# Two pairs of modulation units instead of one in three output passes, and six more half product units

## The reference

```
mod = silu(c) @ w_mod[l] + b_mod[l]                    # 9 x 1024 values for each layer, once for c, once for c_ctx
h   = rmsnorm(x, ng[0]) * (1 + m(1)) + m(0)
gu  = h @ ffn_wi                                       # 1024 -> 2 * 2816
x   = x + 0.5 * m(2) * rmsnorm((silu(gu[:, :2816]) * gu[:, 2816:]) @ ffn_wo, ng[1])
```

## Time and profile before

| | |
|---|---|
| median of 3 runs | 3053.07 us (3049.8 to 3058.28) |
| the profiled execution | 3051.59 us |
| its span, first to last instruction | 3049.8 us |
| TensorE busy | 2910.4 us (95%) |
| VectorE busy | 2166.0 us (71%) |
| ScalarE busy | 1294.8 us (42%) |
| mean granted TensorE clock | 0.981 of full speed |

### The profile page before, as it was taken

One profiled execution on the slowest core, in us unless ns is written; L12 is line 12 of the kernel. 1 busy time (PEld: TensorE's weight loads), 2 busy tenths in 40 slices (PEclk: granted clock), 3 DMA queues, 4 the chain that ended last, 5 costly groups with the idle time before them and its releaser, 6 DMA issues.

```text
span 3049.8 us, 62386 instructions
## 1 busy us (share of the span) xinstructions
PE 2910.4 (95%) x26152; PEld 2601.7 (85%) x26152; DVE 2166.0 (71%) x3223; ACT 1294.8 (42%) x2165; POOL 416.7 (14%) x465
## 2 busy tenths in 40 slices
PE   6999999999988899999999999999998889999998
PEld 5999878996777689998799998799876777999986
DVE  4987586756666788876878776767566767787635
ACT  3135454235533451454532554532454435345434
POOL 1000111002333220001100001110033333100100
PEclk8999999999989999999999999999998999999999
DMA  6522444410000244225452225453010004312234
GB/s 250 201 70 84 152 153 152 179 46 27 30 4 14 99 173 166 70 70 187 145 193 90 90 70 200 145 177 130 15 52 8 3 13 161 111 70 84 83 124 172
DMA packets 92915, 325.10 MB, mean 107 GB/s; under 512 B 10288, under 2 KB 13936, under 8 KB 77296
## 3 DMA queue, kind: packets, MB, share of 16 engines
q1 hardware_dynamic: 92656, 321.39, 29.7%
HBM read 318.05 MB, written 3.31 MB: 105 GB/s over the span
## 4 chain that ended last, share of the span: by engine, by line
PE 80%; DVE 10%; ACT 3%; issue 3%; DMA 3%; POOL 0%; SPq 0%; ACTq 0%; DVEq 0%; POOLq 0%
PE PS L2606 22%; PE PS L2672 20%; PE PS L2719 18%; PE PS L2616 3%; PE PS L812 2%; DMA wo<-in_wo 2%; PE PS L1584 2%; PE PS L836 1%; PE PS L1563 1%; DVE wo_lo L3131 1%; ACT wo_hi L2838 1%; PE PS L759 1%; PE PS L1576 1%; DMA wm<-in_wm 1%; PE PS L824 1%
## 5 line engine op out<-in xcount | busy, mean ns | idle before, releaser
L2606 PE MATMUL PS<-h_hi,wi_hi 128*128 128x384 f32 (+2 forms) x1632 | 406.8, 311 | 11.2 <-issue 11.2
L2719 PE MATMUL PS<-wo_hi,a_hi 128*128 128x512 f32 x968 | 391.6, 405 | 19.3 <-DVE wo_lo L3131 12.7
L2606 PE MATMUL PS<-h_hi,wi_lo 128*128 128x384 f32 (+2 forms) x1632 | 403.8, 309 | 0.0
L2606 PE MATMUL PS<-h_lo,wi_hi 128*128 128x384 f32 (+2 forms) x1632 | 403.7, 309 | 0.0
L3131 DVE TENSOR_TENSOR wo_lo<-wo,wo_hi 128x1024 fp32r<-128x1024 f32 x208 | 255.4, 1228 | 193.2 <-ACT wo_hi L2838 192.6
L2719 PE MATMUL PS<-wo_hi,a_lo 128*128 128x512 f32 x968 | 378.6, 391 | 0.0
L2719 PE MATMUL PS<-wo_lo,a_hi 128*128 128x512 f32 x968 | 378.0, 390 | 0.0
L2838 ACT ACTIVATE wo_hi<-wo 128x1024 fp32r<-128x1024 f32 x208 | 220.2, 1059 | 304.8 <-PE PS L2719 206.6
L3191 DVE TENSOR_TENSOR part_lo<-wi,part_hi 128x512 fp32r<-128x512 f32 x378 | 255.5, 689 | 105.2 <-ACT part_hi L2872 102.2
L2872 ACT ACTIVATE part_hi<-wi 128x512 fp32r<-128x512 f32 x378 | 236.1, 630 | 190.5 <-PE PS L2672 118.8
L2606 PEld LDWEIGHTS PS<-h_hi,wi_hi 128*128 128x128 f32 (+1 forms) x1632 | 262.4, 188 | 15.4 <-issue 13.4
(11 more groups left out here) (370 smaller groups left out, 5813.2 us busy)
## 6 DMA issues: line engine op xcount, KB each, us to landing
wi<-in_wi SPq DMA_DIRECT2D x88, 1024.0 KB, 4.8
wo<-in_wo SPq DMA_DIRECT2D x176, 512.0 KB, 3.2
wm_in<-in_wm SPq DMA_DIRECT2D x104, 512.0 KB, 3.7
wi<-in_win SPq DMA_DIRECT2D x24, 1024.0 KB, 5.2
wo<-in_wout SPq DMA_DIRECT2D x32, 512.0 KB, 3.2
wm_out<-in_wm SPq DMA_DIRECT2D x24, 512.0 KB, 4.4
wm<-in_wm SPq DMA_DIRECT2D x4, 2048.0 KB, 17.7
wq<-in_wq SPq DMA_DIRECT2D x2, 1024.0 KB, 4.7
```

The lines of the kernel that those rows point to most:

```text
L2606: mm = pe.matmul(PSF[0:cols, at:at + GW[g]], st, h[:, k, GA[g]:GA[g] + GW[g]], start=(k == 0 and q == 0), stop=(k == KD - 1 and q == 2))
L2719: mm = pe.matmul(PS[:, OUT_BANK[t] + half, :], a, w[:, (V0(n) + b) % 2, kk, :], start=(u == 0 and kk == 0 and q == 0), stop=True, skip_gro ...
```

## The change

```diff
-MOD_SHARES = {0: (MOD_FIRST, 6), "out0": (10, 2), 1: (12, 4), 2: (16, 6), "out2": (22, 2), 3: (24, 4), "out3": (28, 2),
+MOD_SHARES = {0: (MOD_FIRST, 4), "out0": (8, 4), 1: (12, 4), 2: (16, 4), "out2": (20, 4), 3: (24, 2), "out3": (26, 4),
               4: (30, 4), 5: (34, 2)}
...
-OUT_LOAD = {2: 0, 3: 1, 5: 2, 7: 3, 9: 4, 11: 5, 13: 6, 15: 7}
+OUT_LOAD = {b: b - 2 for b in range(2, 2 + 2 * KD)}
...
-FAST = {0: 10, 2: 10, 3: 8, 5: 6}
+FAST = {0: 8, 2: 8, 3: 6, 5: 6}
...
-        mred_out = place("mred_out", [P, 2, 2, MOD_UNIT * P // QUAD], at_sg + 8 * MOD_UNIT * P)
+        mred_out = place("mred_out", [P, 4, 2, MOD_UNIT * P // QUAD], at_sg + 8 * MOD_UNIT * P)
...
                     if out_mods(n) and b >= OUT_MOD:
-                        mod_ops(dve, out_mods(n), b - OUT_MOD, b - OUT_MOD + 1)
+                        mod_ops(dve, out_mods(n), 2 * (b - OUT_MOD), 2 * (b - OUT_MOD) + 2)
```

## The result

| | before | after |
|---|---|---|
| median, 7 runs of each on one chip | 3055.49 us | 3065.74 us (3063.62 to 3069.44) |
| the profiled execution | 3051.59 us | 3065.74 us |
| its span | 3049.8 us | 3063.9 us |
| TensorE busy | 2910.4 us | 2909.0 us |
| VectorE busy | 2166.0 us | 2203.3 us |

The change makes the kernel slower by 10.2 us: the ratio is 1.0033, with an interval of 1.0022 to 1.0045.

A forecast was written before the change was run, and what follows sets the result against it. TensorE was taken to bound the kernel, with VectorE's spare time in the output passes in question. -10.6 us for six units and +18.9 us for three passes gave +8.3 us, 3061.4 us, range 3057 to 3068 us.

The forecast's parts named there:

- the likeliest of its cases: Whole kernel: gain of the units plus VectorE's delay in three output passes gives 3061.4 us; chance 0.79.
- Six units, -10.6 us: Feed-forward input parts: six plain units of 14.08 us become half product units of 12.32 us, 1.76 us each.
- The sums that left the input parts, nothing: Stages 0, 2 and 3: a pair less for VectorE and SyncE costs or gains nothing, as VectorE idles there.
- The stall, +6.30 us a pass: First output passes: VectorE's steps from slot 10 take 53.13 us, so slot 21 starts 6.30 us later; three passes, +18.9 us.
- full lengths: Rival, output passes: back-to-back VectorE steps wait for the previous end; delay 9.3 us a pass, 3070.3 us; chance 0.07.
- TensorE never feels it: Rival, slots 10 to 21: VectorE's work fits into 46.8 us, leaving only the gain, 3042.5 us; chance 0.06.
- Loads come late: Rival: doubled w_mod loads delay wo at slot 6 and between 12 and 16, 2.6 us a pass, 3069.2 us; chance 0.08.
- The total, +8.3 us: Whole kernel: -10.6 and +18.9 us on the profiled 3051.59 us; as a median 3061.4 us against 3053.07.

The follow-up runs named there:

- e2: Changed kernel with the modulation steps of the three output passes on 128 of 1024 columns, all loads kept: 3043.48 us, ratio 0.9964.
- e10: e2 with the FAST pace table of the kernel before (10, 10, 8), so no added half product units: 3054.87 us, ratio 1.0006.
- e1: Changed kernel with the old FAST pace table (10, 10, 8), the moved pairs kept: 3070.42 us, ratio 1.0051.
- e8: Changed kernel measured again, unaltered, beside another set of runs of the kernel before: 3066.31 us, ratio 1.0033.
- e6: Changed kernel with the modulation operations spread unevenly from slot 2 on, fewer around the cuts in slots 12 and 14: 3057.07 us, ratio 1.0012.
- e9: Kernel before, unchanged, profiled once more: span 3048.9 us.
- e7: e5 with the modulation operations spread from slot 2 to slot 20 to suit it: 3053.18 us, ratio 0.9999.
- e3: Changed kernel with the two cuts of the next stage's wi in slots 7 and 9 instead of 12 and 14: 3073.59 us, ratio 1.0064.
- e5: e3 with ScalarE's cut of wi_hi issued ahead of its gate copy in feed-forward stages: 3060.54 us, ratio 1.002.

## Why the prediction was right

The forecast was the likeliest of its cases, and its steps can be set against the runs one by one.

**Six units, -10.6 us: held.** In stage 0 a half product unit takes 314.71 - 302.39 = 12.32 us in the changed kernel. e2, where apart from the loads nothing else is left of the change, is 10.3 us under before by the medians; e10 against e2 gives 11 to 13, the changed kernel against e1 5 to 6.

**The sums that left the input parts, nothing: held.** e1 has no added unit, and its first stage reaches the step at the output part at 342.31 us, before at 342.76. Its plain units still end 164.07 - 149.99 = 14.08 us apart on VectorE's timeline, though VectorE now idles 9.99 us ahead of that step, where it was 2.62 and 3.42:

```profile
149.99 0.89 DVE L3123 TENSOR_TENSOR act<-sg,PS 128x384 f32<-128x384 f32 x2 [9.99 <-ACT sg L2829]
...
164.07 0.88 DVE L3123 TENSOR_TENSOR act<-sg,PS 128x384 f32<-128x384 f32 x2 [9.99 <-ACT sg L2829]
```

**The stall, +6.30 us a pass: held, to 0.1 us.** It was a sum over VectorE's steps from the `wo_lo` of slot 10 on, 53.13 us; the trace has 53.05. Slot 12 was to stall 1.9 us and stalled 1.92. The split over the slots was good too: 0.6, 0.3, 1.6, 0.3 and 1.6 us were forecast for slots 13 to 16 and 21, and e8 shows 0.59, 0.31, 1.65, 0.32 and 1.4. That the clock would fall in one execution and cover two of these waits was not foreseen; it didn't change the sum. What made the sum good is that it was taken from start to start: 11 steps of 1.14, 16 of 1.195, and the folds with the waits of reduction and transpose for each other. The *full lengths* rival gave 9.3 us a pass and is refuted by the same timeline: two sums last 2.48 us and the next step begins 2.39 after them. The Trainium skill's rule on this ("VectorE: DVE Perf Modes", "The DRAIN you can't avoid") also says that a next operation that isn't held starts earlier. The trace after agrees with that half, as the trace before did.

**TensorE never feels it: refuted.** It decided at 46.8 us of VectorE's work; there were 53.05. e2 shows what would have happened below that point.

**Loads come late: refuted at the size given, but not nothing.** The prediction put the loads at nothing. e2 and e10 have the doubled loads, and both have slots 9 to 20 in one piece of 48.99 us. At slot 6 of stage 0, however, TensorE now waits for `wo`. The chain of waits of the kernel after, and below it TensorE's timeline at that slot:

```profile
353.96 9.12 DMA wo<-in_wo
```

```profile
365.48 0.50 PE L2719 MATMUL PS<-wo_hi,a_hi 128*128 128x512 f32 x1 [0.96 <-DVE wo_lo L3131]
```

Slot 6 begins 1.98 us after the gate row ahead of it, where it was 0.86: 1.1 us. Before, such a wait stood in stage 2, and the chain of stage 0 had none at slot 6. From the `wo_lo` of slot 2 to that of slot 9 stage 0 takes 1.2 us more than before, and 0.8 to 1.2 in e1, e2 and e10, so this goes with the added loads. (In e6, where the sums start a slot earlier, it is 0.2.) The time from the step that opens the output part to slot 7 grows by only 0.2 us, from 31.56 to 31.79, because a wait of TensorE of 0.87 us for the last step at line 3263, at 346.33 in the kernel before, is gone. In stage 3 the same distance is 0.7 us longer in the changed kernel and as before in e1 and e10. The second place that the rival named, between slots 12 and 16, shows nothing.

A second place was not foreseen at all. In the second pass, where the change has no load and no step, one `wo` lands 1.2 us later. ScalarE's timeline in the kernel before, late in the second pass:

```profile
485.75 1.06 ACT L2838 ACTIVATE wo_hi<-wo 128x1024 fp32r<-128x1024 f32 x1 [1.23 <-DMA wo<-in_wo]
```

The same step of the kernel after:

```profile
489.63 1.06 ACT L2838 ACTIVATE wo_hi<-wo 128x1024 fp32r<-128x1024 f32 x1 [2.44 <-DMA wo<-in_wo]
```

It costs TensorE 0.89 us of idle time at 492.01, 1.22 in the changed kernel's other execution, 0.86 in e2, and nothing in either execution of before. From slot 21 to the step at line 3426 the changed kernel takes 91.31 us, the kernel before 90.22. The output part of stage 5, whose code the edit doesn't touch, has such a late load too, and there it goes with the pace table and not with the pairs: 166.7 to 166.9 us in the four executions with the old table (before, e9, e1, e10), 167.0 to 168.6 in the eight with the new one. In the kernel after, the load is in the chain of waits, and a window of the DMA view over 3008 to 3009 us shows a packet of the queue that loads instructions in the middle of it:

```profile
3007.47 4.25 DMA wo<-in_wo
```

```profile
q8 instruction: 1, 0.02, 5.8%
```

In e8 and e2 the same load takes 4.19 and 4.26 us with such a packet under it, and the late one of stage 0 has one as well. In both executions of before no such packet falls between 2986 and 3003 us, where that load stands, and loads in the chain around it take 3.2 to 3.4 us. So a changed program may load its instructions at other moments, and under other loads. That is a likely cause that no run has tested.

**The total, +8.3 us: 2 us short.** The median moved by 10.2 us, and by 12.1 in the second comparison; the interval of 6.7 to 13.7 us holds the 8.3. What is missing from the sum has the sign and the size of the surplus seen in the output parts and in the piece with mixer 1, where one slot alone has 1.6 us of it (last section). In the same way e7 should have gained 3 x 1.50 - 10.6 = -6.1 against before and shows 0 to -1: it matches its sum against the changed kernel (-13.1 for -14) and carries the same surplus against before. The mechanism was right and the sum lacks these small terms; the loads, put at nothing, are one of them, with 1.1 us at slot 6 of stage 0. What the rest is made of in each of the stages stays open. That the forecast of the total came this close is in part luck: the profiled executions differ by 14.1 and 16.2 us, and the forecast of 3061.4 us, which stood on a median of 3 runs, is 4.3 us under the measured 3065.74.

The edit, then, is a bad trade: it buys 10.6 us and pays 18.6, since the pairs went into the one place of the stage where VectorE has other fixed work.

## What to carry to other kernels

Whether an engine has room is a question about a stretch, not a share: VectorE was idle for 21.8 of 79 us, yet between slots 10 and 21 there was no room for a second pair in this order. Write down the engine's steps of the stretch from start to start, with what waits for what, and compare their sum with the time that the bounding engine leaves; that came within 0.1 us of 53 here. Before a step moves to an emptier slot, look what it lands behind on each engine in order: the same cut cost some 9.6 us against the changed kernel behind a wait (e3) and gained 5.8 ahead of it (e5).

## What the runs showed that was not expected

**TensorE's clock after short stalls.** The granted clock fell to the 1.2 GHz level after some stalls of about 2 us and not after others. Windows of 5 us over the first pass (busy us, records, granted clock, DMA share, GB/s), kernel after:

```profile
385.00:390.00 5.00, 5.00 (x24) 1.00 0.85 286
390.00:395.00 5.00, 3.08 (x15) 1.00 0.35 137
395.00:400.00 5.00, 5.00 (x15) 0.66 0.62 210
```

The last of these windows in the kernel's other execution, e8:

```profile
395.00:400.00 5.00, 4.71 (x21) 1.00 0.75 234
```

Both have a stall of 1.92 us ahead of slot 12, and only the first has the lower clock behind it. It cost nothing here, since slot 15 had to wait for VectorE in any case. In mixer 1 it did cost. The chain of waits of before, at a slot in front of which TensorE waits for the cut of a weight:

```profile
1060.52 4.40 PE PS L2719 x18
```

The same slot in the kernel after, behind the same wait:

```profile
1065.04 5.98 PE PS L2719 x18
```

And in e8:

```profile
1065.16 6.03 PE PS L2719 x18
```

TensorE's wait ahead of it is 1.87 us in all of them, and the windows of the kernels before and after show a clock of 1.00 and of 0.66. The program is the same in this place, and yet the difference repeats: the second execution of before has 4.41 us, e1 and e3 have 6.01 and 5.99, the six other kernels 4.39. Two executions of each program agree, which speaks for the program and against chance, though two are few. So some 1.6 us of the surplus in the piece with mixer 1 probably belong to the changed program. Why the clock falls there in some kernels and not in others isn't shown.

Other pieces do differ between executions of one program, as mixer 4 with 858.50 and 861.34 us. So a comparison of two single profiles has an error of a few us that doesn't come from the edit, here 14.1 and 16.2 us between profiles for 10.2 and 12.1 between medians.
